# Recurrent stage: the quarters of a projection's weight block stand in pairs in the order, in place of one by one between the small products

## What is computed

```python
def rwkv7_step(state, inp):
    r_t, w_t, k_t, v_t, kk_t, a_t = inp
    sa = jnp.einsum('bhvk,bhk->bhv', state, -kk_t)
    state = (state * w_t[:, :, None, :]
             + sa[..., None] * (kk_t * a_t)[:, :, None, :]
             + v_t[..., None] * k_t[:, :, None, :])
    y = jnp.einsum('bhvk,bhk->bhv', state, r_t)
    return state, y
...
        if l % 2 == 0:
            z = h @ even_w_in[j]
            a_val, a_glu, a_gate, r, k, v, wd, ad, b_gate = split_cols(z, EVEN_SIZES)
            ya = conformer_conv(a_val, a_glu, conv_w[j], conv_vec[j]) * jax.nn.silu(a_gate)
            yb = rwkv7_mix(r, k, v, wd, ad, rwkv_mu_rkv[j], rwkv_mu_lora[j], rwkv_vec[j],
                           rwkv_w_up[j], rwkv_a_up[j], rwkv_r_k[j]).astype(h.dtype)
            yb = yb * jax.nn.silu(b_gate)
            out = jnp.concatenate([ya, yb], axis=-1) @ even_w_out[j]
```

## Time and profile before

| what | value |
|---|---|
| median of 3 runs | 2866.38 us (2862.49 to 2867.17) |
| span of the profiled execution | 2861.7 us |
| PE busy | 2696.6 us, 94% |
| DVE, ACT, POOL busy | 78%, 42%, 46% |
| 24-quarter rounds 2 to 6 | about 71.4 us each, from 203.6 to 560.6 us of the span |
| whole stretch of rounds 0 to 9 | from about 74 to 745 us of the span |

### The profile page before, as it was taken

The page is one execution under the profiler, slowest core; times in us unless marked ns, Lnnn a source line. Parts: engine busy times, 40 slices in busy tenths (PEclk is TensorE's granted clock), DMA queues, the critical chain, the costliest instruction groups (busy, mean ns, idle before and its releaser), DMA issues.

```text
span 2861.7 us, 36860 instructions
## 1 busy us (share of the span) xinstructions
PE 2696.6 (94%) x14355; PEld 2238.5 (78%) x14355; DVE 2243.3 (78%) x3548; ACT 1208.4 (42%) x1794; POOL 1326.9 (46%) x859
## 2 busy tenths in 40 slices
PE   8889999999999999999999998999999999999887
PEld 4567777767777788787788988999888888777775
DVE  3688888876878987657569999993777788889875
ACT  3234444443533467733334435664333333333334
POOL 2233333322234544204344766445676776667730
PEclk9999999999999999999999999999999999999998
DMA  7321111134422221023233444777999999999971
GB/s 275 107 70 52 52 52 52 52 118 150 145 74 74 81 67 45 30 89 111 82 102 103 155 156 128 232 245 268 363 372 356 366 359 334 329 329 331 327 262 37
DMA packets 163165, 496.09 MB, mean 173 GB/s; under 512 B 15152, under 2 KB 50992, under 8 KB 162864
## 3 DMA queue, kind: packets, MB, share of 16 engines
q1 hardware_dynamic: 126128, 359.51, 37.4%
q0 software_dynamic: 36864, 134.23, 12.6%
HBM read 443.87 MB, written 49.81 MB: 173 GB/s over the span
## 4 chain that ended last, share of the span: by engine, by line
PE 53%; DVE 27%; DMA 8%; ACT 6%; issue 3%; POOL 3%; SPq 0%; DVEq 0%; ACTq 0%; POOLq 0%
PE ps L800 14%; PE ps L802 14%; PE ps L801 14%; DMA ex<-in_ev,small 4%; DVE oh L2561 3%; DVE ex L1794 2%; DVE ex L2595 2%; PE ps L973 2%; DVE oh L2558 1%; DMA ex<-in_urow,small 1%; DVE oh L2556 1%; DVE pk L2487 1%; PE ps L993 1%; POOL ex L2848 1%; PE ps L947 1%
## 5 line engine op out<-in xcount | busy, mean ns | idle before, releaser
L2682 POOL TENSOR_TENSOR wsp<-ring,wsp 128x1024 fp32r<-128x1024 f32 x219 | 561.1, 2567 | 849.4 <-ACT wsp L1302 823.9
L800 PE MATMUL ps<-hT,wsp 128*128 128x512 f32 (+1 forms) x2040 | 780.8, 383 | 44.2 <-POOL wsp L2682 23.6
L802 PE MATMUL ps<-hT,wsp 128*128 128x512 f32 (+1 forms) x2040 | 752.6, 369 | 0.0
L801 PE MATMUL ps<-hT,wsp 128*128 128x512 f32 (+1 forms) x2040 | 751.7, 368 | 0.0
L800 PEld LDWEIGHTS ps<-hT,wsp 128*128 128x128 f32 x2040 | 387.8, 190 | 117.0 <-issue 32.3
L802 PEld LDWEIGHTS ps<-hT,wsp 128*128 128x128 f32 x2040 | 387.5, 190 | 47.0
L801 PEld LDWEIGHTS ps<-hT,wsp 128*128 128x128 f32 x2040 | 388.5, 190 | 44.2 <-issue 5.0
L1302 ACT ACTIVATE wsp<-ring 128x1024 fp32r<-128x1024 f32 x317 | 331.9, 1055 | 152.0 <-PE ps L802 80.0
L800 PE MATMUL ps<-ex 128*128 128x512 f32 x588 | 233.4, 397 | 29.6 <-DVE ex L1794 26.4
L2848 POOL DMA_INDIRECT ex<-in_ev,small x128 | 194.3, 1518 | 101.1 <-DVE ex L2595 87.6
L2848 POOL DMA_INDIRECT ex<-in_urow,small x128 | 197.8, 1545 | 84.0 <-DVE small L2588 69.4
(11 more groups left out here) (429 smaller groups left out, 5020.5 us busy)
## 6 DMA issues: line engine op xcount, KB each, us to landing
ring<-in_eu SPq DMA_DIRECT2D x128, 512.0 KB
ring<-in_ev SPq DMA_DIRECT2D x128, 512.0 KB
ring<-in_ein SPq DMA_DIRECT2D x57, 512.0 KB
gd<-oh SPq DMA_DIRECT2D x6, 4096.0 KB, 14.2
ex<-gd SPq DMA_DIRECT2D x32, 768.0 KB
ring<-in_oin SPq DMA_DIRECT2D x39, 512.0 KB
ring<-in_ada SPq DMA_DIRECT2D x30, 512.0 KB
ex<-zd SPq DMA_DIRECT2D x20, 768.0 KB, 9.6
```

Source lines behind the costliest of these rows:

```text
L800: pe.matmul(out, W[0], R[0], start=first, stop=False)
L801: pe.matmul(out, W[0], R[1], start=False, stop=False)
L802: return pe.matmul(out, W[1], R[0], start=False, stop=last)
L2682: pool.tensor_tensor(s[:, 1, :], raw_of(i), s[:, 0, :].bitcast(F32), ALU.subtract).then_inc(pool_done, G.step("lo", i))
```

## The change

`spread` gives places to the lane of the projection. Before, item j stood at (j + 0.5) of the lane's length. Now an even quarter takes (j + 1.0) and the odd quarter behind it keeps that same place, so that quarters 0 and 1 stand together, and 2 and 3. Other items (`ada`, `turned`) keep their places. Quarters 0 and 2 come half a step later, quarters 1 and 3 half a step earlier. No instruction is added or removed; the pieces are the same, in another order on every engine.

```diff
 def spread(items):
-    return [(1000 * (j + 0.5) / len(items), x) for j, x in enumerate(items)]
+    out, n = [], 0
+    for j, x in enumerate(items):
+        if not (x[0] == "dense" and x[3] % 2):
+            n = j + (1.0 if x[0] == "dense" else 0.5)
+        out.append((1000 * n / len(items), x))
+    return out
```

## The result

The changed kernel takes **2974.52 us** (2966.4 to 2979.84, 4 runs), beside 2866.78 us for the kernel before on the same chip: a ratio of 1.0376, 95% interval 1.0354 to 1.0397. The prediction was 2925 us, with a range of 2898 to 2946. The direction was right, and so was most of the mechanism; the size was not: 108 us in place of 59.

What follows compares the result with a forecast made beforehand. TensorE's stream of matmuls was taken as the bound, so uncovered waits add fully: 40 us for five rounds, 14 for others, 5 for clock, on 2861.7 plus 4.7 us around the span, giving 2925 us (2898 to 2946).

Steps and rivals of the forecast that it cites:

- the prices of rounds 7 to 9: Uncovered waits in the last rounds, priced as in the regular ones: 4.5, 4 and 1.5 us.
- second ab behind VectorE: Round's end: second ab waits for VectorE's u, reciprocal, gn4 and bank copies, 3.0 us a round.
- second turn behind the sigmoid, less u's wait: Round's end: first turn's copy queues behind the sigmoid, delaying the second turn 1.0 us; u's 0.55 us wait goes.
- p2 then p1, last p2 then tr: Small products left without a quarter between wait for VectorE: 0.95 and 0.45, together 1.4 us a round.
- tr then p1: At the start, p1 waits for GpSimd's two copies after tr, 1.15 us a round.
- sa then st: st waits for ScalarE's copy: 0.5 us each for chunks 0 and 2, 0.25 for chunk 3, total 1.3.
- x1, and odd then p2: x1 of chunk 2 waits for chunk 1's state, 1.0 us; p2 after odd at level 1, 0.5; together 1.5.
- fewer switches: Quarter runs fall from 22 to 12, saving switches to small products on TensorE: about -0.8 us a round.
- gn4 2.26: Round's end, VectorE: gn4, queued behind u and ahead of the copies, takes 2.26 us, read from the earlier trace.
- I take half of the lower price: 5: Clock loss after waits at six round ends, between nothing and 2.1 us each; 5 us in all.
- rival of a falling clock at every round's end: Clock falls at each round's end, costing 2.1 us or more: 54 + 20, 2941 us; chance 0.17.
- the first rival: New waits hide one another, short ones shrinking by two thirds: 4.5 us a round, 2893 us; chance 0.17.

Runs made afterwards that it cites:

- filler run: Changed kernel plus 20 matmuls of 128x512, results unread, ahead of the second ab in rounds 1 to 6: 2972.17 us, 1.0359.
- run with u first: Kernel before, but in rounds 2 to 6 VectorE takes glu's product u ahead of the last reciprocal and gn4: 2898.07 us, 1.0103.
- Holding GpSimd back: Changed kernel, but GpSimd begins the low half made at r's second quarter only once gn4 is done: 2967.7 us, 1.035.
- u behind gn4: Changed kernel, but VectorE takes glu's product u behind the last reciprocal and gn4; TensorE's order unchanged: 2947.38 us, 1.0289.
- 5.0 and no other pairs: Kernel before, but with glu's last two quarters and r's first two in pairs: 2907.86 us, 1.0143.
- Taking it away alone: Changed kernel, but bgate's last two quarters stand one by one as before: 2968.95 us, 1.0356.
- run of all pairs but those at the end: Changed kernel, but glu's last two quarters and r's first two stand one by one: 2935.29 us, 1.0247.
- their own run: Kernel before, but with quarters in pairs in rounds 7 to 9 alone: 2897.8 us, 1.0114.

## Why the prediction was wrong in size, step by step

In rounds 2 to 6 three steps failed: the duration of gn4, the price of the clock, and the path, which left out the wait at odd. Outside them the prices of rounds 7 to 9 failed, and that is the largest part.

Per round 3 to 6, forecast against measured, in us (round 2 has no wait at odd and lost less to the clock, 10.7 in all):

| step of the prediction | forecast | measured | from |
|---|---|---|---|
| second ab behind VectorE | 3.0 | 5.0 | row L952 |
| second turn behind the sigmoid, less u's wait | 1.0 - 0.55 | 0.7 - 0.55 | row L936 |
| p2 then p1, last p2 then tr | 1.4 | 1.1 | rows L978 (DVE), L966 |
| tr then p1 | 1.15 | 0.9 | row L978 (POOL) |
| sa then st | 1.3 | 0.7 | row L1033 |
| x1, and odd then p2 | 1.5 | 0.7 | rows L1010, L998 |
| odd behind bgate's silu | none | 1.3 | row L988 |
| fewer switches; TensorE's busy time at full clock | -0.8 | +1.1 | 71.85 against 70.8 in the earlier trace rows |
| clock | 0.8 | 2.7 | filler run |
| sum | 8.8 | 13.6 | round: 13.7 |

**The end of the round.** The step that failed here is "gn4 2.26 (343.17 to 345.72 less the 0.29 idle)". Up to there the chain was right: from u's start to the end of the first ab's slot the prediction had 2.2, and it is 2.22 (538.56 to 540.78). From u to the second ab it had 5.2 and it is 7.25; of the 2.05 us between, 2.02 are L2095 at 2.71 in place of 0.69. I took gn4 from a place where GpSimd was idle and moved it, without asking what GpSimd does at the new place; where I did look at GpSimd's halves of the weights, I had "No cost". (It is gn4's move that makes them meet: in the run with u first, GpSimd has its order of before.) Holding GpSimd back restored 0.69 and the wait of 3.0. The trace of before had the same thing to show: on VectorE L1987 of prep, of the same shape, took 1.54 us in round 3 beside a low half, and it too ended 0.54 us behind it:

```profile
318.39 1.54 DVE L1987 SCALAR_TENSOR_TENSOR rw<-rw,vec 128x512 f32<-128x512 f32 x1
317.01 2.38 POOL L2682 TENSOR_TENSOR wsp<-ring,wsp 128x1024 fp32r<-128x1024 f32 x1 [2.36 <-ACT wsp L1302]
```

Three pairs of rows, 0.54, 0.55 and 0.54. They are no exceptions: in the kernel before, up to 760 us, 18 operations TENSOR_TENSOR or SCALAR_TENSOR_TENSOR of 128x512 on VectorE with both inputs in SBUF began while a TENSOR_TENSOR of GpSimd was under way, and all ended 0.55 to 0.57 us behind it, while 65 taps (L1970, one input in PSUM) that began beside one took 0.75 to 0.76 us, which is their usual time.

The Trainium skill, page SBUF — State Buffer, section Who interferes with whom, states that a VectorE instruction with two inputs in SBUF contends with a GpSimd instruction that reads SBUF, and that the one which comes second is blocked until the first is through. The rows agree: L2095, L2092 and L1987 have both inputs in SBUF and began after GpSimd's, and 540.93 L2089, which began before it, kept its 0.75. By that page the meeting could have been looked for, and by the row of 318.39 it could have been priced.

**The clock.** The step "I take half of the lower price: 5" failed. The filler run puts 11.6 us on it in rounds 2 to 6, about 2.7 in each of the last four, where 4 were forecast for them. The clock over 10 us around the end of a round is 1.00 with a wait of 1.5 us at ab (u behind gn4), 0.83 with 3.0 (GpSimd held back), the lower price of the earlier trace rows, and 0.66 with 5.0 in the changed kernel (545 to 555 us). But the length of that wait alone doesn't settle it: with 5.0 and no other pairs the clock is 0.83 in one run and with 4.9 and no pairs at all 0.66 in the other (508 to 518 us of the run with u first), and with the pair of r between the two ab and a wait of only 2.1 it is 0.53. What decides between them is open. The rival of a falling clock at every round's end was right for rounds 2 to 6, and with it, at 20 us, the sum would have been 2941.

**Odd behind bgate** was overlooked. bgate's quarters, paired, bring ScalarE's table load of 1.28 us ahead of the copy that odd waits for. And this load isn't hidden: ScalarE begins it when bgate's last matmul is done (512.21 us), where glu's load was over before:

```profile
512.21 1.28 ACT L1431 ACT_TABLE_LOAD   x1 [2.57 <-PE ps L807]
```

Taking it away alone gains nothing, since p2 is next in line, so it isn't simply additive, though the sum of the table needs it.

**The short waits and the switches.** The short waits were all there but one: the third sa then st is covered by odd's new wait. They add up to 4.1 us in place of 6.35, but that is mostly a matter of counting. The forecast counted from the end of a product's slot, the trace counts idle time from the end of its last matmul, and that is about 0.2 us later, as rows of before show: sa has a slot of 0.47 and a duration of 0.66, tr 0.85 and 1.09, p2 0.81 and 1.05, turn 0.36 and 0.60. Measured from start to start, in round 5, turn to turn is 1.34 us (537.73 to 539.07; forecast 1.36), tr to p1 1.97 (2.0), sa to st 1.02 (0.97) and p2 to p1 1.92 (1.76). So these four were right to within 0.2 us, and the first rival, which had the short waits shrink by two thirds, was wrong.

The same 0.2 us stands in TensorE's busy time, since nothing overlaps the last matmul before a wait. At full clock TensorE is busy 71.85 us in a round with u behind gn4 and 71.7 to 71.8 in the run of all pairs but those at the end, against 70.8 in the earlier trace rows, with the same instructions. Three waits behind sa and one each behind turn, tr and p2 account for some 1.3 us by the rows above, an estimate. So the +1.1 in the table is no loss by switches; what fewer switches gained can't be read from it, and no run tells.

**The other rounds.** Here lies the largest part of the miss: priced at 14 us, and one more for the clock, they cost 37. For rounds 7 to 9, 10 us was forecast and 32.2 measured by their own run. There, "turn after turn 1.0" was 2.1 in round 7 (ScalarE loads a table in between, 643.43 to 644.71 us, which it begins only when the quarter before is done), and the waits at x1 (2.0) and p2 (1.6) of round 7 and at p2 (2.2) and st (1.5) behind it were not in my list: I had carried over prices from rounds 2 to 6, whose lane has other kinds between the same products, and had not gone through these orders closely enough. The clock is the other part, 3.8 and 4.7 us. Round 1 is 6.6 for 4.

Together: 65.6 us in rounds 2 to 6 against 44 forecast with the clock, of which 10 are VectorE held up by GpSimd, 5 the wait at odd, and 11.6, where 4 were forecast, the clock; and 37 in the others against 15. Of the two signs that the prediction named for a wrong size, one came: gn4 does not end before the sigmoid, but the clock at the rounds' ends is well under 0.83. The last 5 us of the miss of 49 lie between the execution that was profiled, the fastest, and the median.

## What to carry to other kernels

When work is moved, look up not only what it waits for but what the neighbour engines do at its new place: a duration read from one place (0.69 us) needn't hold at another (2.71 us beside a GpSimd operation). Uncovering a round trip on an engine that is never idle cost its full length here, counted from start to start, and the queue of an engine with slack decided how long it was: one waiting product ahead of a reciprocal and the three operations of gn4 on VectorE cost 6.3 to 7.0 us a round by itself. Rounds with another mix of work have to be gone through one by one; prices carried over from the regular ones were short by a factor of three in rounds 7 to 9 (10 us against 32).

## What the hardware showed that I had not expected

A VectorE operation of 128x512 with both inputs in SBUF, which takes 0.69 to 0.75 us alone, took 2.71 and 2.87 us beside GpSimd's subtraction of 128x1024, and ended 0.54 to 0.55 us behind GpSimd's end; VectorE's taps, with one input in PSUM, kept their 0.75 us beside it. Waits of 5.0 us at the end of each round brought the granted clock to 0.51 over the 7 us from 545 us, at which the second ab took 2.08 in place of 1.13 us; matmuls that fill the wait kept it at 1.00.
